# Delta-rule decay rows: a column turned with step zero instead of two fp32 products with replicated columns

## The chip, the cores and the metric

The kernel runs on one core of a Trainium2 chip, as one launch. The metric is the time of that launch on the device in microseconds, the median of several runs. Everything is float32, and matrix products are done either on plain fp32 operands or, in the projections and experts, as three products of rounded high and low parts.

## What is computed

Two layers on 512 tokens of width 1024, each a mixer and a mixture of 16 experts. The mixer of the first layer holds, beside a gated linear attention, a gated delta rule of 4 heads of width 128 in chunks of 64 tokens. The change lies there:

```
def gated_delta_chunked(q, k, v, g, beta):
    b = jnp.cumsum(g, axis=-1)
    ...
    gamma = jnp.exp(jnp.where(incl, b[..., :, None] - b[..., None, :], -jnp.inf))
    k_beta = k * beta[..., None]
    a_low = jnp.where(strict, jnp.einsum('bhnid,bhnjd->bhnij', k_beta, k) * gamma, 0.0)
    ...
    sol = lax.linalg.triangular_solve(eye + a_low, rhs, left_side=True, lower=True, unit_diagonal=True)
    ...
    qk = jnp.einsum('bhnid,bhnjd->bhnij', q, k) * gamma
    q_dec = q * jnp.exp(b)[..., None]
```

The norms of q and k are folded into the exponents: the kernel keeps log factors lk, lq and lbk (for k, q, and beta times k) per token and head. The matrix under the exponential, for token j on the partitions and token i along the row, is (b_i + lbk_i) + (lk_j - b_j) for the triangular system and (b_i + lq_i) + (lk_j - b_j) for q·k. The part with j is a column, which VectorE adds as a scalar per partition (`colj`). The part with i is needed as a row that is the same on all 128 partitions. These are the decay rows.

## The kernel before, in words

The kernel is written per engine: TensorE, VectorE (`dve`), ScalarE (`act`), GpSimd (`pool`) and SyncE (`sp`, which issues most DMAs) each run their own program in the order of the code, and named semaphores tell one engine that another has done a step. Between stages every compute engine counts up `phase_done` and waits for all (a barrier). Tokens are handled in 4 tiles of 128 (two chunks each, t = 0..3), and each tile has 4 heads, so that a tile of 4 x 128 columns fills one PSUM bank.

The delta-rule stage begins at the barrier `phase_done` 3 * 2. Ahead of it, within the linear-attention stage, `gdn_pre_gates` and `gdn_pre` (VectorE, L2211 to L2239) make the per-token columns: the log factors, and from a product of g with the triangular constant `tri` the running sums b, of which `pre[:, 1]` = b + lbk and `colj` = lk - b are kept.

The stage's own order of work:

- `gdn_inverses` (all 4 tiles). VectorE writes, per tile, g and lbk replicated over 128 columns per head into xx and xt (L2320, L2321). TensorE makes the decay rows of each tile, two fp32 products per head that add up in one bank (replicated g times `tri`, L1136; replicated lbk times identity, L1137), then k·k of the tile (L1140). VectorE adds colj and a mask (L2325, the decay step), ScalarE takes the exponential, VectorE multiplies by k·k (L2331) and makes first operands for all four tiles (L2334, L2337, L2341). TensorE turns x0 (L937, called at L1145), then five levels of inverse products follow (L1155, L1160, L1163) with VectorE's updates (L2348, L2350, L2351) and side sums for the modulation (L2062).
- `gdn_rows(0)`, `gdn_kq(0)`, `gdn_kv(0)`, `gdn_solve(0)`: decay rows of tile 0 for q·k (L1170, L1171), q·k (L1178), turned k and v (L937), and the solve (L1193, L1195). The replicated columns for these rows are made by ScalarE (`gdn_rep`, L1761 to L1768). VectorE clears ku_b (L2866), then waits for the turned k and v (L2385).
- `gdn(t)`, t = 0..3, the recurrence over two chunks c. On TensorE per chunk: product with the state (L1228), something that prepares tile t+1 (for c = 0 `gdn_rows(t + 1)`, for c = 1 `gdn_kv(t + 1)`), then the state's update (L1246), which waits for VectorE's vn (L2415). VectorE then forms the new state (L2423). ScalarE's `gdn(t)` runs the sums of squares of tile t-1 (`gdn_root`), the exponentials and copies of tile t+1, and `gdn_rep(t + 2)` at the end.

At the stage's end stands the barrier 3 * 3, after which SP starts to fetch the experts' weights (L765) and TensorE starts the output projection (L1286).

The helper `turn(dst, src)` (L936) is TensorE's transpose of src with the identity: src is the stationary operand that is loaded, the identity the moving one. In the profile names a product's moving operand comes first, so a turn of a tile in `work` reads `ps<-const,work`. All of ScalarE's activations are issued by one helper line, L1576.

Of the kernel before, what the change touches and what calls it, by code (L numbers as in the profile page):

```python
# [15 lines left out]
P = 128  # L16
SEQ, D = 512, 1024
TT = SEQ // P
# [98 lines left out]
def build_block(nc, a, out):  # L117
    ctx = ExitStack()
    with ctx:
        def sem(name):  # L120
            return ctx.enter_context(nc.semaphore(name))
# [154 lines left out]
        tiles, levels = range(TT), range(1, 6)  # L276
        MAT_PE = Steps(sem("gdn_mat_pe"), [f"{n}{t}" for t in tiles for n in ("rows", "kk")] + [f"x0{t}" for t in tiles])
        MAT_ACT = Steps(sem("gdn_mat_act"), [f"{n}{t}" for n in ("exp", "x0") for t in tiles])
        MAT_DVE = Steps(sem("gdn_mat_dve"), [f"{n}{t}" for n in ("rep", "d", "at", "level0", "xt0", "level1") for t in tiles])
        INV_PE = Steps(sem("gdn_inv_pe"), [f"{n}{l}{t}" for l in levels for n in ("p", "y") for t in tiles])  # L280
        INV_ACT = Steps(sem("gdn_inv_act"), [f"p{l}{t}" for l in levels for t in tiles])
        INV_DVE = Steps(sem("gdn_inv_dve"), [f"{n}{l}{t}" for l in levels for t in tiles
                                             for n in (("xt", "x", "level") if l < 5 else ("xt", ))])

        GDP_PE = Steps(sem("gdn_prep_pe"), ["rows", "kq", "kv", "uw"])
        GDP_ACT = Steps(sem("gdn_prep_act"), ["rep", "exp", "eq", "wT", "u"])
        GDP_DVE = Steps(sem("gdn_prep_dve"), ["kb", "vb", "d", "qk", "qd", "ku"])
        GDN_DVE = Steps(sem("gdn_dve"), ["vn0", "s0", "vn1", "s1"])
        GDH_DVE = Steps(sem("gdn_norm_dve"), ["zg", "var", "n1", "n2", "n3", "rstd", "on"])
# [134 lines left out]
        gla_end = top["work"]  # L424

        top["work"] = 0
        rep = carve("work", 2, HEADS, P)
        ex = carve("work", HEADS, P)
        xt = carve("work", TT, HEADS, P)
        kb_b = carve("work", HEADS, P)  # L430
# [14 lines left out]
        pzb = carve("work", TT, 512)  # L445
        psm = carve("work", TT, 24)
        qkvT = carve("work", 12, 3 + SEQ)
        pre_u = carve("work", TT, 8)
        pre_a = carve("work", TT, 8)
        pre_l = carve("work", TT, 8)  # L450
# [174 lines left out]
        def cols(t):  # L625
            return slice(P * t, P * t + P)
# [306 lines left out]
        def _(pe):  # L933
# [197 lines left out]

            def gdn_inverses():
                for t in range(TT):
                    pe.wait_ge(MAT_DVE.sem, MAT_DVE.at(0, f"rep{t}"))
                    for hd in range(HEADS):
                        mm(bank(t)[:, cols(hd)], xx[:, t, hd], cst("tri"), start=True, stop=False)  # L1136
                        ins = mm(bank(t)[:, cols(hd)], xt[:, t, hd], ident, start=False, stop=True)  # L1137
                    ins.then_inc(MAT_PE.sem, MAT_PE.one(f"rows{t}"))
                    for hd in range(HEADS):
                        ins = mm(bank(4 + t)[:, cols(hd)], qkvT[:, 4 + hd, tok(t)], qkvT[:, 4 + hd, tok(t)], start=True, stop=True)  # L1140
                    ins.then_inc(MAT_PE.sem, MAT_PE.one(f"kk{t}"))
                for t in range(TT):
                    pe.wait_ge(MAT_DVE.sem, MAT_DVE.at(0, f"xt0{t}"))
                    for hd in range(HEADS):
                        ins = turn(bank(t)[:, cols(hd)], xt[:, t, hd])  # L1145
                    ins.then_inc(MAT_PE.sem, MAT_PE.one(f"x0{t}"))
                for l in range(1, 6):
                    for t in range(TT):
                        if l == 1:
                            pe.wait_ge(MAT_ACT.sem, MAT_ACT.at(0, f"x0{t}"))  # L1150
                            pe.wait_ge(MAT_DVE.sem, MAT_DVE.at(0, f"level1{t}"))
                        else:
                            pe.wait_ge(INV_DVE.sem, INV_DVE.at(0, f"level{l - 1}{t}"))
                        for hd in range(HEADS):
                            ins = mm(bank(t)[:, cols(hd)], lev_at[:, t, hd], xx[:, t, hd], start=True, stop=True)  # L1155
                        ins.then_inc(INV_PE.sem, INV_PE.one(f"p{l}{t}"))
                    for t in range(TT):
                        pe.wait_ge(INV_ACT.sem, INV_ACT.at(0, f"p{l}{t}"))
                        for hd in range(HEADS):
                            ins = mm(bank(4 + t)[:, cols(hd)], pm[:, t, hd], xt[:, t, hd], start=True, stop=True)  # L1160
                        if l < 5:
                            for hd in range(HEADS):
                                ins = mm(bank(t)[:, cols(hd)], xt[:, t, hd], pm[:, t, hd], start=True, stop=True)  # L1163
                        ins.then_inc(INV_PE.sem, INV_PE.one(f"y{l}{t}"))
                pe.wait_ge(INV_DVE.sem, INV_DVE.at(0, f"xt5{TT - 1}"))

            def gdn_rows(t):
                pe.wait_ge(GDP_ACT.sem, GDP_ACT.at(t, "rep"))
                for hd in range(HEADS):
                    mm(bank(1)[:, cols(hd)], rep[:, 0, hd], cst("tri"), start=True, stop=False)  # L1170
                    ins = mm(bank(1)[:, cols(hd)], rep[:, 1, hd], ident, start=False, stop=True)  # L1171
                ins.then_inc(GDP_PE.sem, GDP_PE.one("rows"))

            def gdn_kq(t):
# [399 lines left out]
        def _(act):  # L1574
            def f(out, in_, fn=ACT.Copy, **kw):
                return nc.scalar.activation(out, in_, fn, **kw)  # L1576
# [181 lines left out]
                            act.wait_ge(INV_PE.sem, INV_PE.at(0, f"y{l - 1}{t}"))  # L1758
                        f(pm[:, t], bank(t, HEADS, P)).then_inc(INV_ACT.sem, INV_ACT.one(f"p{l}{t}"))

            def gdn_rep(t):  # L1761
                if t:
                    act.wait_ge(GDP_PE.sem, GDP_PE.at(t - 1, "rows"))
                else:
                    act.wait_ge(PRE_DVE.sem, PRE_DVE.at(0, "lq"))
                for n, src in enumerate((g_b, lq)):
                    ins = f(rep[:, n], src[:, t].unsqueeze(2).to_broadcast([P, HEADS, P]))
                ins.then_inc(GDP_ACT.sem, GDP_ACT.one("rep"))  # L1768

            def gdn_prep(t):  # L1770
                b = t % 2
                act.wait_ge(GDP_DVE.sem, GDP_DVE.at(t, "d"))
# [22 lines left out]
            def gdn(t):  # L1795
                ahead = t + 1 < TT
                if t:
                    gdn_root(t - 1)
                if ahead:
                    table(ACT.Exp)  # L1800
                    gdn_prep(t + 1)
                else:
                    put_mod(0, 0, 4)
                if t:
                    put_output_b(t - 1)
                if ahead:
                    gdn_solve(t + 1)
                if t + 2 < TT:
                    gdn_rep(t + 2)
                if ahead:  # L1810
                    table(ACT.Abs_reciprocal_sqrt)

# [177 lines left out]
            gla()  # L1990
            nc.scalar.drain().then_inc(phase_done, 1)
            act.wait_ge(phase_done, 3 * 2)
            gdn_rep(0)
            table(ACT.Exp)
            gdn_inverses()
            gdn_prep(0)
            gdn_solve(0)
            gdn_rep(1)
            for t in range(TT):
                gdn(t)  # L2000
            gdn_root(TT - 1)
# [32 lines left out]
        def _(dve):  # L2034
# [194 lines left out]
            def gdn_pre():  # L2229
# [3 lines left out]
                v.tensor_copy(pre[:, 0], lnb)  # L2233
                v.tensor_tensor(pre[:, 1], cum[:, 0], lbk, ALU.add)
                v.tensor_tensor(pre[:, 2], cum[:, 1], lk, ALU.add)
                v.tensor_copy(pre[:, 3:5], cum[:, 2:4]).then_inc(D_.sem, D_.one("pre"))
                v.tensor_tensor(colj, lk, cum[:, 0], ALU.subtract).then_inc(D_.sem, D_.one("colj"))
                dve.wait_ge(D_.sem, D_.at(0, "colj"))
# [77 lines left out]

            def gdn_inverses():

                for t in range(TT):
                    v.tensor_copy(xx[:, t], g_b[:, t].unsqueeze(2).to_broadcast([P, HEADS, P]))  # L2320
                    v.tensor_copy(xt[:, t], lbk[:, t].unsqueeze(2).to_broadcast([P, HEADS, P])).then_inc(MAT_DVE.sem, MAT_DVE.one(f"rep{t}"))  # L2321
                for t in range(TT):
                    dve.wait_ge(MAT_PE.sem, MAT_PE.at(0, f"rows{t}"))
                    for hd in range(HEADS):
# [606 lines left out]
```

## Time and profile before

| | us |
|---|---|
| median of 3 runs | 1470.79 |
| lowest, highest | 1470.17, 1473.98 |
| span of the profiled execution | 1464.9 |
| TensorE busy in it | 1280.1 (87%) |
| VectorE busy | 1101.5 (75%) |
| ScalarE busy | 693.7 (47%) |
| mean granted TensorE clock | 0.924 |
| delta-rule stage in it, from its barrier to the next | about 309 to 449 |

The span runs from the first to the last instruction of one profiled execution; for the profiled execution no other time is given than its span, which lies 5.9 us below the median of the runs. Matmuls are pipelined: the records of successive ones overlap, so the distance from start to start is the pace, not a record's length. An fp32 product of this size shows as two records, a turn as one. In a timeline, neighbouring instructions of one line are put together: start, time to the last one's end, how many records, and in brackets the idle time ahead with what ended it.

### The profile page before, as it was taken

What the parts mean: (1) busy time and instruction counts of PE and PEld (TensorE: products, weight loads), DVE (VectorE), ACT (ScalarE), POOL (GpSimd) and SP (SyncE); (2) the same over time, 40 slices, a digit from 0 to 9 for tenths busy, and PEclk for the clock granted to TensorE, in tenths of its full rate; (3) what the DMA queues carried; (4) which work ended last, traced back from release to release, by engine and by line L of the source; (5) the groups of instructions that cost most, each with busy time, mean ns of one, the idle gap of its engine ahead of it and who ended that gap; (6) DMA issues with size and microseconds to landing.
All of it is one profiled execution on the core that took longest, in us unless ns stands there. A gap on an engine that the chain in (4) does not pass through costs nothing. (4 is left out here: it accounts for less than half of the span.)

```text
span 1464.9 us, 15502 instructions
## 1 busy us (share of the span) xinstructions
PE 1280.1 (87%) x6000; PEld 970.2 (66%) x6000; DVE 1101.5 (75%) x1324; ACT 693.7 (47%) x890; POOL 311.9 (21%) x129
## 2 busy tenths in 40 slices
PE   4798997859899959999999967986898799999992
PEld 1476885659884557888888754444446588888882
DVE  2757986667783657999999946967357499999994
ACT  2222344222251316777777714227522377777770
POOL 2100000000000001555555310000000145555541
PEclk9799998979999959999999977997996799999997
DMA  9788626011703257999999546354006499999955
GB/s 328 259 266 272 214 96 211 19 44 58 259 2 130 87 219 273 375 391 382 373 378 373 225 157 240 115 203 183 1 29 258 142 358 385 377 381 392 380 206 191
DMA packets 63856, 338.17 MB, mean 231 GB/s; under 512 B 11837, under 2 KB 12350, under 8 KB 49700
## 3 DMA queue, kind: packets, MB, share of 16 engines
q1 hardware_dynamic: 51428, 311.00, 57.3%
q0 software_dynamic: 11536, 22.91, 4.5%
q10 hardware_dynamic: 816, 3.23, 0.6%
q8 instruction: 50, 0.82, 0.2%
q14 instruction: 26, 0.21, 0.0%
HBM read 325.64 MB, written 28.84 MB: 242 GB/s over the span
## 5 line engine op out<-in xcount | busy, mean ns | idle before, releaser
L1421 PE MATMUL ps<-ring_r,work_r 128*128 128x512 f32 x536 | 212.7, 397 | 0.0
L2455 DVE TENSOR_TENSOR ring_r<-ring,early_mod_r 128x2048 fp32r<-128x2048 f32 x76 | 188.7, 2512 | 21.2 <-ACT early_mod_r L1576 20.7
L1419 PE MATMUL ps<-early_mod_r,work_r 128*128 128x512 f32 x468 | 187.8, 401 | 7.7 <-DVE work_r L2758 4.7
L834 POOL TENSOR_TENSOR work<-work,early_mod 128x1024 f32<-128x1024 f32 x30 | 158.1, 5271 | 157.3 <-ACT work L1576 157.3
L1576 ACT ACTIVATE work<-ps 128x512 f32<-128x512 f32 (+3 forms) x121 | 80.5, 670 | 224.8 <-PE ps L1421 134.7
L1420 PE MATMUL ps<-early_mod_r,work_r 128*128 128x512 f32 x468 | 183.1, 391 | 0.0
L1576 ACT ACTIVATE work_r<-ring 128x2048 fp32r<-128x2048 f32 (+2 forms) x87 | 133.8, 1558 | 89.2 <-PE ps L946 89.2
L1576 ACT ACTIVATE early_mod_r<-ring 128x2048 fp32r<-128x2048 f32 x79 | 147.6, 1910 | 0.3 <-PE ps L1421 0.3
L937 PE MATMUL ps<-const,work 128*128 128x128 f32 x712 | 106.4, 293 | 44.2 <-DMA work<-h_rows,row_i 11.9
L1419 PE MATMUL ps<-work_r 128*128 128x512 f32 x324 | 132.9, 410 | 6.8 <-DVE work_r L2758 4.7
L937 PEld LDWEIGHTS ps<-const,work 128*128 128x128 f32 x712 | 90.1, 151 | 68.7 <-issue 15.0
L2455 DVE TENSOR_TENSOR ring_r<-ring,work_r 128x2048 fp32r<-128x2048 f32 x52 | 130.4, 2533 | 1.1 <-ACT work_r L1576 1.1
L1420 PE MATMUL ps<-work_r 128*128 128x512 f32 x324 | 128.9, 398 | 0.0
L1421 PEld LDWEIGHTS ps<-ring_r,work_r 128*128 128x128 f32 x536 | 102.7, 192 | 23.1
L1286 PE MATMUL ps<-ring,hT 128*128 128x512 f32 x256 | 111.1, 593 | 1.4 <-ACTq L2025 0.7
L1419 PEld LDWEIGHTS ps<-early_mod_r,work_r 128*128 128x128 f32 x468 | 88.2, 188 | 29.0 <-DVE work_r L2758 8.1
L1420 PEld LDWEIGHTS ps<-early_mod_r,work_r 128*128 128x128 f32 x468 | 88.4, 189 | 17.0
L826 POOL DMA_INDIRECT work<-h_rows,row_i x32 | 57.3, 1790 | 177.9 <-PE ps L937 130.1
L1286 PEld LDWEIGHTS ps<-ring,hT 128*128 128x128 f32 x256 | 48.2, 190 | 60.8 <-issue 58.3
L1310 PE MATMUL ps<-ring,hT 128*128 128x512 f32 x192 | 86.2, 608 | 1.9 <-ACT hT L1576 1.9
L1576 ACT ACTIVATE work_r<-ps 128x512 fp32r<-128x512 f32 (+1 forms) x66 | 53.3, 810 | 66.4 <-PE ps L937 66.4
L1419 PEld LDWEIGHTS ps<-work_r 128*128 128x128 f32 x324 | 62.7, 194 | 23.0 <-DVE work_r L2758 7.7
(330 smaller groups left out, 2448.3 us busy)
## 6 DMA issues: line engine op xcount, KB each, us to landing
ring<-in_moe_w_up_dram SPq DMA_DIRECT2D x33, 2048.0 KB, 10.8
early_mod<-in_ada_w_dram SPq DMA_DIRECT2D x80, 512.0 KB, 4.4
ring<-in_moe_w_gate_dram SPq DMA_DIRECT2D x19, 2048.0 KB, 9.6
hT<-in_moe_w_down_dram SPq DMA_DIRECT2D x16, 2048.0 KB, 9.9
ring<-in_moe_w_down_dram SPq DMA_DIRECT2D x15, 2048.0 KB, 10.2
work<-in_moe_w_gate_dram SPq DMA_DIRECT2D x14, 2048.0 KB, 10.8
ring<-in_ab_w_in_dram SPq DMA_DIRECT2D x7, 2048.0 KB, 10.4
ring<-in_ada_w_dram SPq DMA_DIRECT2D x4, 2048.0 KB, 23.6
```

Of the source, the lines that this page charges most:

```text
L826: nc.gpsimd.indirect_dma_start(xg[buf], None, h_rows[l], bass.IndirectOffsetOnAxis(rows_, 0), bounds_check=SEQ - 1, oob_is_err=False).then ...
L834: return nc.gpsimd.tensor_tensor(yb[buf], yb[buf], mod[:, 5 * D:6 * D], ALU.mult)
L937: return nc.tensor.transpose(dst, src, ident[0:k, 0:k])
L1286: ins = mm(bank((2 * t + n) % 3), oT[:, k, cols(t)], slot(c0 + n)[:, k], start=(k == 0), stop=(k == 7))
L1310: ins = mm(bank(j % 4), hT[:, k, cols(t)], slot(c)[:, k], start=(k == 0), stop=(k == 7))
L1419: mm(out, a_lo, w_hi, start=first_, stop=False)
L1420: mm(out, a_hi, w_hi, start=False, stop=False)
L1421: return mm(out, a_hi, w_lo, start=False, stop=last_)
L1576: return nc.scalar.activation(out, in_, fn, **kw)
L2455: v.tensor_tensor(half_of(l, m, half, True), half_of(l, m, half), highs[(2 * m + half) % MHIGHS].bitcast(F32), ALU.subtract).then_inc(SV.s ...
```

## The change

The decay rows are made otherwise. `pre[:, 1]`, the column b + lbk per token and head, exists already; a new column `colq` = b + lq is made beside it with one addition. A decay row tile for a head is then the transpose of a 128 x 128 view of that single column, read with step zero along the columns: `turn(bank, column.to_broadcast([P, P]))`. This replaces the two fp32 products per head in `gdn_inverses` (16 heads x tiles) and in `gdn_rows` (another 16). The replicated copies go: eight of VectorE's in `gdn_inverses`, and the eight activations of ScalarE's `gdn_rep`, with the waits of TensorE for both. The tile `rep` is no longer carved; `colq` lies in free columns of `psm`.

```diff
-        MAT_DVE = Steps(sem("gdn_mat_dve"), [f"{n}{t}" for n in ("rep", "d", "at", "level0", "xt0", "level1") for t in tiles])
+        MAT_DVE = Steps(sem("gdn_mat_dve"), [f"{n}{t}" for n in ("d", "at", "level0", "xt0", "level1") for t in tiles])
...
-        GDP_ACT = Steps(sem("gdn_prep_act"), ["rep", "exp", "eq", "wT", "u"])
+        GDP_ACT = Steps(sem("gdn_prep_act"), ["exp", "eq", "wT", "u"])
...
-        rep = carve("work", 2, HEADS, P)
...
+        colq = psm[:, :, 0:HEADS]
...
             def gdn_inverses():
                 for t in range(TT):
-                    pe.wait_ge(MAT_DVE.sem, MAT_DVE.at(0, f"rep{t}"))
                     for hd in range(HEADS):
-                        mm(bank(t)[:, cols(hd)], xx[:, t, hd], cst("tri"), start=True, stop=False)
-                        ins = mm(bank(t)[:, cols(hd)], xt[:, t, hd], ident, start=False, stop=True)
+                        ins = turn(bank(t)[:, cols(hd)], pre[:, 1, t, hd:hd + 1].to_broadcast([P, P]))
...
             def gdn_rows(t):
-                pe.wait_ge(GDP_ACT.sem, GDP_ACT.at(t, "rep"))
                 for hd in range(HEADS):
-                    mm(bank(1)[:, cols(hd)], rep[:, 0, hd], cst("tri"), start=True, stop=False)
-                    ins = mm(bank(1)[:, cols(hd)], rep[:, 1, hd], ident, start=False, stop=True)
+                    ins = turn(bank(1)[:, cols(hd)], colq[:, t, hd:hd + 1].to_broadcast([P, P]))
...
-            def gdn_rep(t):
-                if t:
-                    act.wait_ge(GDP_PE.sem, GDP_PE.at(t - 1, "rows"))
-                else:
-                    act.wait_ge(PRE_DVE.sem, PRE_DVE.at(0, "lq"))
-                for n, src in enumerate((g_b, lq)):
-                    ins = f(rep[:, n], src[:, t].unsqueeze(2).to_broadcast([P, HEADS, P]))
-                ins.then_inc(GDP_ACT.sem, GDP_ACT.one("rep"))
-
...
-                if t + 2 < TT:
-                    gdn_rep(t + 2)
...
-            gdn_rep(0)
...
-            gdn_rep(1)
...
                 v.tensor_tensor(pre[:, 2], cum[:, 1], lk, ALU.add)
+                v.tensor_tensor(colq, cum[:, 0], lq, ALU.add)
...
             def gdn_inverses():
 
-                for t in range(TT):
-                    v.tensor_copy(xx[:, t], g_b[:, t].unsqueeze(2).to_broadcast([P, HEADS, P]))
-                    v.tensor_copy(xt[:, t], lbk[:, t].unsqueeze(2).to_broadcast([P, HEADS, P])).then_inc(MAT_DVE.sem, MAT_DVE.one(f"rep{t}"))
```

TensorE in the recurrence at t = 0, from the product with the state to its update, before. Behind a line stands the semaphore it waits for: `gdn_prep_act` is ScalarE's, `gdn_prep_dve` and `gdn_dve` are VectorE's.

```order
L1228 MATMUL ps<-work,ring 64x128 [waits gdn_prep_act]
L1228 MATMUL ps<-work,ring 64x128 x3
L1170 MATMUL ps<-early_mod,work 128x128 [waits gdn_prep_act]
L1171 MATMUL ps<-const,work 128x128
...
L1246 MATMUL ps<-work,ring 128x128 [waits gdn_prep_dve,gdn_dve]
L1246 MATMUL ps<-work,ring 128x128 x3
```

The same place in the changed kernel, whose line numbers are 4 lower (L1228 is L1224 there, L1246 is L1242):

```order
L1224 MATMUL ps<-work,ring 64x128 [waits gdn_prep_act]
L1224 MATMUL ps<-work,ring 64x128 x3
L937 MATMUL ps<-const,work 128x128 x4
L1242 MATMUL ps<-work,ring 128x128 [waits gdn_prep_dve,gdn_dve]
L1242 MATMUL ps<-work,ring 128x128 x3
```

Eight products with a wait for ScalarE have become four turns with none; nothing else stands between the two lines.

## Rows read from the trace of the kernel before

**Rows 1.** Timeline, ScalarE then VectorE at the barrier (start us, us, engine line op)
```profile
308.53 0.60 ACT L1576 ACTIVATE hT<-ps 128x512 f32<-128x512 f32 x1 [0.43 <-PE ps L937]
309.29 1.15 ACT L1576 ACTIVATE work<-work 128x512 f32<-128x512 f32 x2 [0.17 <-ACTq L1991]
...
309.87 0.48 DVE L2863 MEMSET work<- 128x512 f32 x1
310.39 0.43 DVE L2320 COPY ring<-work 128x512 f32<-128x512 f32 x1
```

**Rows 2.** Timeline, TensorE in the first decay rows and k·k
```profile
311.30 0.76 PE L1136 MATMUL ps<-early_mod,ring 128*128 128x128 f32 x2 [2.81 <-DVE work L2321]
...
314.84 1.91 PE L1140 MATMUL ps<-work 128*128 128x128 f32 x8
316.55 0.60 PE L1136 MATMUL ps<-early_mod,ring 128*128 128x128 f32 x2
...
323.91 1.06 PE L1140 MATMUL ps<-work 128*128 128x128 f32 x8
```

**Rows 3.** Timeline, VectorE, decay steps of the first and last tile
```profile
315.09 1.12 DVE L2325 SCALAR_TENSOR_TENSOR ring<-ps,work,early_mod 128x128 f32<-128x128 f32 x4 [1.92 <-PE ps L1137]
...
324.11 1.12 DVE L2325 SCALAR_TENSOR_TENSOR ring<-ps,work,early_mod 128x128 f32<-128x128 f32 x4 [1.55 <-PE ps L1137]
325.15 1.28 DVE L2331 TENSOR_TENSOR ring<-ps,ring 128x512 f32<-128x512 f32 x2
```

**Rows 4.** Windows of 1 us: engines' busy time, then PEclk, DMA share, GB/s
```profile
316.00:317.00 1.00, 1.00 (x7) 1.00 (x7) 0.21 (x1) 0.63 (x1) 0.00 (x0) 0.51 0.00 0
317.00:318.00 1.00, 1.00 (x11) 1.00 (x11) 0.00 (x0) 0.00 (x0) 0.00 (x0) 1.00 0.00 0
...
333.00:334.00 1.00, 1.00 (x7) 1.00 (x6) 1.00 (x3) 0.75 (x2) 0.00 (x0) 0.50 0.00 0
334.00:335.00 1.00, 1.00 (x11) 1.00 (x10) 0.84 (x2) 0.74 (x2) 0.00 (x0) 0.98 0.00 0
```

**Rows 5.** Timeline, TensorE then VectorE, decay rows of tile 0 for q·k
```profile
385.07 0.49 PE L1170 MATMUL ps<-early_mod,work 128*128 128x128 f32 x2 [0.78 <-DVE work L2348]
...
387.86 1.04 PE L937 MATMUL ps<-const,work 128*128 128x128 f32 x8
...
385.39 1.76 DVE L2866 MEMSET ring<- 128x2048 f32 x1 [0.38 <-issue]
388.93 0.69 DVE L2385 TENSOR_TENSOR work<-ps,work 128x512 f32<-128x512 f32 x1 [1.77 <-PE ps L937]
```

**Rows 6.** Timeline, TensorE then VectorE, recurrence at t = 0 and 1
```profile
394.53 0.49 PE L1170 MATMUL ps<-early_mod,work 128*128 128x128 f32 x2 [0.43 <-ACT work L1576]
...
396.42 1.06 PE L1246 MATMUL ps<-work,ring 128*128 128x128 f32 x8
...
408.95 1.06 PE L1246 MATMUL ps<-work,ring 128*128 128x128 f32 x8
...
394.67 0.68 DVE L2415 TENSOR_TENSOR work<-ring,ps 64x512 f32<-64x512 f32 x1
...
407.57 0.68 DVE L2415 TENSOR_TENSOR work<-ring,ps 64x512 f32<-64x512 f32 x1
408.93 0.17 DVE L2394 TENSOR_SCALAR work<-work 128x4 f32<-128x4 f32 x1 [0.68 <-ACT early_mod L1576]
```

**Rows 7.** Timeline, TensorE, turns of x0 and first inverse products
```profile
330.69 3.58 PE L937 MATMUL ps<-const,work 128*128 128x128 f32 x16 [5.72 <-DVE work L2337]
334.11 3.73 PE L1155 MATMUL ps<-ring 128*128 128x128 f32 x32
```

**Rows 8.** Timeline, VectorE, end of the decay preparation
```profile
261.52 0.16 DVE L2237 TENSOR_TENSOR work<-work,ps 128x16 f32<-128x16 f32 x1
263.48 1.28 DVE L2062 SCALAR_TENSOR_TENSOR x<-early_mod,par,x 128x1024 f32<-128x1024 f32 x1 [1.80 <-issue]
```

**Rows 9.** Timeline, SP's queue, first expert weights
```profile
448.83 0.33 SPq L765 DMA_DIRECT2D ring<-in_moe_w_gate_dram  x1
```

## The prediction

> **What bounds the kernel now.** I read the views from the outside in. The chain that ended last covers only the final DMA and adds, so it says nothing of this stage; I took the windows table and then the timeline of each engine over the delta-rule stage, from about 309 us to 449 us of the span. What matters there is which wait ends last at each of the four places where decay rows are made.
>
> At the entry, ScalarE's last copy of the stage before starts at 308.53 and takes 0.60, and its next work starts at 309.29 [rows 1]. That barrier releases everybody. VectorE then clears two tiles and writes eight replicated tiles (L2320, L2321); TensorE's first product starts at 311.30, released by the first L2321 [rows 1, 2]. So 2 us pass between barrier and product, for operands only. Then TensorE is the bound: the decay step of VectorE (L2325) is idle before each tile and released by L1137 each time; the last tile's step starts at 324.11, and everything behind it on VectorE is back to back [rows 3]. The pitch is slow because the granted clock is 0.50 until 317, 1.00 after [rows 4], that is 1.2 and then 2.4 GHz, 5.7 us after the first product.
>
> At the second place, TensorE makes the decay rows of tile 0 (L1170, L1171) from 385.07, then queues k·q and the turned k and v behind them; VectorE has finished clearing ku_b (385.39 + 1.76 = 387.15) and waits 1.77 us for the turned k and v [rows 5]. In the loop, the rows of tile t+1 stand between the product with the state (L1228) and the state's update (L1246) on TensorE. They start at 394.53 after waiting 0.43 us for ScalarE's replica and the update starts at 396.42, whereas VectorE had its operand at 394.67 + 0.68 [rows 6].
>
> **The change part by part.** The price of the new operation first. A turned 128x128 tile is one record where an fp32 product is two: 8 turns take 1.04 us at full clock with the last one's tail, 0.11 us each, and the 16 from 330.69 to the next line's 334.11 at half clock, 0.21 us each [rows 5, 7]. Two fp32 products are 4 records: the eight products of a tile take 394.53 to 396.42, 1.89 us with 0.1 us of entry [rows 6]. So one tile's decay rows go from 1.79 us to 0.45 us at full clock, 0.85 us at half clock. No row shows a turn whose source has step zero. From below it can't cost less than the 0.11 us pitch, since the identity still streams through the array; from above the nearest rows are these ordinary turns, and the farthest the products it replaces, 0.45 us per head. I take the ordinary turn. The Trainium skill (SBUF — State Buffer, Door 1: The DMA port swizzle) says repeated accesses to one 16-byte line run at full bandwidth, which a step of zero would satisfy; no run here shows it yet.
>
> *Entry and first rows.* VectorE's eight copies and TensorE's wait for them go. TensorE starts at 309.4 instead of 311.30 (0.1 us after the barrier at 309.3). In front of the last decay step stand 4 groups of turns and 3 groups of k·k; a k·k group is 1.71 us at half clock (314.84 to 316.55) and 0.9 us at full (eight of the 32 records that take 3.73 us) [rows 2, 7]. At half clock throughout this is 4 x 0.85 + 3 x 1.71 + 0.4 of pipeline tail = 8.9 us, so the last step starts at 318.3: 5.8 us earlier than 324.11. If the clock rises 5.7 us after the first turn, as it did here, the 2.8 us of work left shrink to 1.5, it starts at 316.8: 7.3 us earlier. If it rises 3.4 us after (as it did behind the turns of 330.69, below), at 315.8: 8.3 us earlier. TensorE was last busy just before the barrier, closer than now, so I take the middle of the last two, **7.8 us**. VectorE isn't a new bound: tile 0's rows are ready at 310.65, after its two clears (309.87 + 0.48 = 310.35), and a step of 1.12 us per tile is shorter than TensorE's 1.3 to 2.6 us per tile [rows 1, 3].
>
> *Second climb of the clock.* Between the stages TensorE waits 5.72 us for VectorE and starts the turns of x0 at half clock; 3.4 us later the clock is up [rows 4, 7]. After the change the distance may be anything from 3.4 to 5.7 us, and up to 2.3 us of work at half clock costs up to 1.1 us more. I take **0.5 us back**.
>
> Here the trace contradicts a rule. Between 324.97 and 334 TensorE did nothing but 16 turns, and the window 333 to 334 shows 0.50, 334 to 335 shows 0.98 [rows 4, 7]: turns alone had raised the clock. The Trainium skill (TensorE: Matmul & The Clock Gate, Part 4: PE-mode transpose) says that transposes don't count as busy and the fast clock doesn't engage for them. The row decides for the sum; by the rule it would be 7.3 us (rival A).
>
> *Rows of tile 0.* 1.79 - 0.45 = **1.34 us**. Whole, because VectorE's cover, the clearing of ku_b, ends 1.77 us before the operands come [rows 5].
>
> *Loop, tiles 1, 2, 3.* Here VectorE's vn takes over as what ends last, so the 1.34 us don't count whole. For t = 0 the update starts at 394.67 + 0.68 + 0.05 = 395.40 instead of 396.42: **1.02 us** (TensorE's rows would be done at 394.4). For t = 1 vn starts at 407.57, so the update starts at 408.30 instead of 408.95: **0.65 us** [rows 6]. The next turn of the loop has the same pattern 12.9 us later (one more **0.65 us**). The last has no rows to make. ScalarE loses its replicas (two activations of 1.15 us together, four times), and so begins its sums of squares earlier; before, VectorE waited 0.68 us for them at 408.93, after vn and before the update's result [rows 6]. The update's result now comes at 408.30 + 1.06 = 409.36, still behind that addition's end at 409.10, and without the replica ScalarE is 1.15 us earlier besides. It costs nothing.
>
> *Added.* One VectorE addition, colq, of the kind of L2237 (0.16 us), in the decay preparation. VectorE is idle for 1.80 us right behind it, waiting for ScalarE's exponentials [rows 8]; if that cover were gone, it would cost 0.1 us.
>
> Sum: 7.8 - 0.5 + 1.34 + 1.02 + 0.65 + 0.65 = 11.0 us. It reaches the end, since SP issues the first expert weights at 448.83, behind the barrier that ends this stage [rows 9], so the whole weight stream moves with it. The side weights fetched in the stage are paced by VectorE's own use of them. The profiled execution has a span of 1464.9 us, and the median of the runs shown is 5.9 us above that, so I subtract from the median: 1470.8 - 11.0 = **1459.8 us**, or 1453.9 us of span.
>
> **The rivals.**
> *A, the clock stays low in the first stage.* k·k is half or more of the work there and might be broken up too much by turns. Then the first term is 5.8. If the turns of x0 don't raise it either, the inverse products behind them run at half clock for the 3.4 to 5.7 us that a climb takes, which costs half of that, 2.2 us in the middle: 5.8 - 2.2 + 3.66 = 7.3 us, 1463.5 us. For it: the first climb took 5.7 us here with products alone; against it: turns alone made the second [rows 2, 4, 7]. 8%.
> *B, it isn't worth what it frees.* The gain is there at 449 us but is lost in later stages to clock climbs that fall otherwise, each at most some 1 us as above; it would take seven of them to come below 4.4 us. The three runs differ by 3.8 us. About 1467. 5%.
> *C, slower: the weight load with step zero.* All 128 columns of a load read one address of each partition. If that serialises, a turn's load no longer hides under the products. All 32 turns stand in TensorE's queue ahead of a waiting engine. The 11.0 us are gone when each costs 0.34 us more, some 0.45 to 0.55 us for a turn, four times the ordinary one; at eight times, 0.9 us, it would be 32 x 0.79 - 11 = 14 us slower, 1485 us. For it: only that no row shows such a read. Against: VectorE reads such columns to make the replicas at 0.43 us for 512 elements, under 1 ns each [rows 1]. 3%.
> That the change doesn't do what it says: TensorE could still wait at the entry, for ScalarE's drain, which the 309.3 already holds; the rows of the loop lose their wait altogether. Included in B.
>
> **How the numbers follow.** The forecast has 84%, within itself 1458.5 to 1462.4 by its bounds (5.8 - 1.1 + 3.66 = 8.4 at the least, 8.3 + 3.66 = 12.0 at the most). With the runs' scatter, and with A, the range is 1457.0 to 1464.3. About 0.3%, 4.4 us, is what a measurement can tell from no change. Faster by more: forecast and A, 0.91. Same: B and the near part of C, 0.06. Slower: 0.03.
>
> **What would show it.** Right: the first turn near 309.4; 16 records of decay rows in the first stage and 16 later, in place of 64 and 64; the last decay step starting near 316; VectorE's idle time before kb shrunk from 1.77 to 0.4 us; the update L1246 released by VectorE and no longer following rows back to back; barrier to SP's first expert load near 438. Wrong: turns further apart than 0.11 us at full clock or loads longer than the ordinary turn's (C); the window from 314 to 318 still at 0.50 (A); SP's load at 438 with an end not 11 us earlier (B).

## The result, and the profile after

The changed kernel takes 1457.38 us (median of 4 runs, 1455.11 to 1460.33) against 1470.48 us for the kernel before (4 runs). The ratio is 0.9909, 95% interval 0.9884 to 0.9933: faster, by 10 to 17 us. The forecast was 1459.8 us in a range of 1457.0 to 1464.3.

| | before, us | after, us |
|---|---|---|
| span of the profiled execution | 1464.9 | 1453.1 |
| TensorE busy | 1280.1 | 1271.0 |
| VectorE busy | 1101.5 | 1098.0 |
| ScalarE busy | 693.7 | 689.7 |
| stage: VectorE's clearing of vn to the output projection's first product | 139.46 | 128.51 |

The stage counts for the whole gain, to within what traces scatter by: the two spans differ by 11.8 us, of which 10.95 lie in the stage, 1.50 ahead of it, and the part behind it is 0.65 longer. Here is the timeline of TensorE in the changed kernel at the entry, which answers to [rows 2, 7]. Columns are start and length in us, engine, line, operands, number of records, and in brackets the idle time ahead with what ended it.

```profile
307.71 1.12 PE L937 MATMUL ps<-const,work 128*128 128x128 f32 x4 [0.72 <-ACTq L1976]
308.62 1.92 PE L1138 MATMUL ps<-work 128*128 128x128 f32 x8
310.33 1.06 PE L937 MATMUL ps<-const,work 128*128 128x128 f32 x4
311.18 1.47 PE L1138 MATMUL ps<-work 128*128 128x128 f32 x8
312.48 0.60 PE L937 MATMUL ps<-const,work 128*128 128x128 f32 x4
312.92 1.06 PE L1138 MATMUL ps<-work 128*128 128x128 f32 x8
313.81 0.60 PE L937 MATMUL ps<-const,work 128*128 128x128 f32 x4
314.25 1.06 PE L1138 MATMUL ps<-work 128*128 128x128 f32 x8
321.03 3.67 PE L937 MATMUL ps<-const,work 128*128 128x128 f32 x16 [5.72 <-DVE work L2318]
324.49 4.31 PE L1153 MATMUL ps<-ring 128*128 128x128 f32 x32
```

TensorE starts 0.7 us behind its last turn of the stage before, released by ScalarE's drain (`ACTq`), and not by a VectorE copy. From start to start four turns take 0.85 to 0.91 us at half clock and 0.44 us at full. The last two rows show the other side: the turns of x0 again start 5.72 us after TensorE went idle, again at half clock.

VectorE at the same place, the counterpart of [rows 1, 3]:

```profile
307.83 0.48 DVE L2843 MEMSET work<- 128x512 f32 x1 [2.01 <-ACTq L1976]
308.37 0.48 DVE L2844 MEMSET work<- 128x512 f32 x1
308.93 1.12 DVE L2306 SCALAR_TENSOR_TENSOR ring<-ps,work,early_mod 128x128 f32<-128x128 f32 x4
311.43 1.13 DVE L2306 SCALAR_TENSOR_TENSOR ring<-ps,work,early_mod 128x128 f32<-128x128 f32 x4 [1.37 <-PE ps L937]
313.12 1.13 DVE L2306 SCALAR_TENSOR_TENSOR ring<-ps,work,early_mod 128x128 f32<-128x128 f32 x4 [0.57 <-PE ps L937]
314.45 1.13 DVE L2306 SCALAR_TENSOR_TENSOR ring<-ps,work,early_mod 128x128 f32<-128x128 f32 x4 [0.20 <-PE ps L937]
```

The first decay step finds its rows ready; the later ones wait less and less, 1.37, 0.57, 0.20 us, where before the four waited 1.92, 2.53, 1.55 and 1.55. TensorE is still the bound, but hardly. The last step starts 6.62 us behind the clearing of vn, before it was 14.78 us (324.11 - 309.33, the start of the first of the two clearings).

The windows of 1 us (engines' busy time, then PEclk, DMA share, GB/s), the counterpart of [rows 4]:

```profile
311.00:312.00 1.00, 1.00 (x6) 1.00 (x5) 0.57 (x3) 0.00 (x0) 0.00 (x0) 0.50 0.13 53
312.00:313.00 1.00, 1.00 (x11) 1.00 (x10) 0.55 (x3) 0.41 (x1) 0.00 (x0) 0.99 0.00 0
...
319.00:320.00 1.00, 0.00 (x0) 0.00 (x0) 1.00 (x3) 0.00 (x0) 0.00 (x0) 0.50 0.00 0
...
325.00:326.00 1.00, 1.00 (x8) 1.00 (x8) 0.18 (x1) 0.34 (x1) 0.00 (x0) 0.66 0.08 16
326.00:327.00 1.00, 1.00 (x12) 1.00 (x11) 0.00 (x0) 0.60 (x1) 0.00 (x0) 1.00 0.00 0
```

The clock rises 4.3 us behind the first turn, between the 3.4 and 5.7 us that bounded the estimate, and the second time some 4.6 us behind the first turn of x0.

Tile 0 and the recurrence, TensorE then VectorE, the counterpart of [rows 5, 6]:

```profile
376.03 0.65 PE L937 MATMUL ps<-const,work 128*128 128x128 f32 x4 [0.78 <-DVE work L2329]
...
383.59 0.65 PE L937 MATMUL ps<-const,work 128*128 128x128 f32 x4
384.96 1.16 PE L1242 MATMUL ps<-work,ring 128*128 128x128 f32 x8 [0.72 <-DVE work L2396]
...
396.95 1.16 PE L1242 MATMUL ps<-work,ring 128*128 128x128 f32 x8 [0.59 <-DVE work L2396]
...
376.35 1.76 DVE L2847 MEMSET ring<- 128x2048 f32 x1 [0.38 <-issue]
378.49 0.69 DVE L2366 TENSOR_TENSOR work<-ps,work 128x512 f32<-128x512 f32 x1 [0.37 <-PE ps L937]
...
396.22 0.68 DVE L2396 TENSOR_TENSOR work<-ring,ps 64x512 f32<-64x512 f32 x1
396.82 0.15 DVE L2375 TENSOR_SCALAR work<-work 128x4 f32<-128x4 f32 x1
```

VectorE's wait for the turned k and v is 0.37 us, from 1.77. The state's update L1242 now waits for VectorE's vn (L2396): the bound has changed hands, as forecast. At that place the variance step (L2375) no longer waits for ScalarE; its fourth and last occurrence still waits 1.73 us, as before. The end of the stage, in SP's queue:

```profile
436.38 0.33 SPq L765 DMA_DIRECT2D ring<-in_moe_w_gate_dram  x1
```

Laid side by side, in pieces that add up to the stage (each from start to start in the timelines):

| piece, us | before | after | measured | forecast |
|---|---|---|---|---|
| clearing of vn to last decay step | 14.78 | 6.62 | -8.16 | -7.8 |
| to TensorE's first update product of the inverses (L1160) | 13.57 | 14.19 | +0.62 | +0.5 |
| to VectorE's last inverse update (L2348) | 46.65 | 46.65 | 0 | 0 |
| to kb of tile 0 (L2385) | 4.60 | 3.20 | -1.40 | -1.34 |
| to the state's first update (L1246) | 7.49 | 6.47 | -1.02 | -1.02 |
| to the first update at t = 2 | 25.44 | 24.36 | -1.08 | -1.30 |
| to the output projection | 26.93 | 27.02 | +0.09 | 0 |
| sum | 139.46 | 128.51 | -10.95 | -10.96 |

### The profile page after: what moved, and what is told of

Read it like the earlier page. It is cut to its first block and busy times, and to the rows that moved or that the text cites. A ratio compares the mean times of both kernels' runs of the same rounds, so it can differ in the third digit from the quotient of the medians.

```text
span 1453.1 us, 15293 instructions
## 1 busy us (share of the span) xinstructions
PE 1271.0 (87%) x5904; PEld 960.4 (66%) x5904; DVE 1098.0 (76%) x1317; ACT 689.7 (47%) x882; POOL 310.5 (21%) x129
## 5 line engine op out<-in xcount | busy, mean ns | idle before, releaser
L2436 DVE TENSOR_TENSOR ring_r<-ring,early_mod_r 128x2048 fp32r<-128x2048 f32 x76 | 193.2, 2572 | 23.7 <-ACT early_mod_r L1572 23.2
L834 POOL TENSOR_TENSOR work<-work,early_mod 128x1024 f32<-128x1024 f32 x30 | 150.4, 5014 | 151.9 <-ACT work L1572 151.9
L937 PE MATMUL ps<-const,work 128*128 128x128 f32 x744 | 114.7, 298 | 45.6 <-DMA work<-h_rows,row_i 11.9
L937 PEld LDWEIGHTS ps<-const,work 128*128 128x128 f32 x744 | 96.0, 153 | 70.8 <-issue 14.9
L2436 DVE TENSOR_TENSOR ring_r<-ring,work_r 128x2048 fp32r<-128x2048 f32 x52 | 126.2, 2451 | 3.4 <-ACT work_r L1572 3.4
L826 POOL DMA_INDIRECT work<-h_rows,row_i x32 | 62.8, 1961 | 186.1 <-PE ps L937 138.1
L830 POOL DMA_INDIRECT y_rows<-work,dest_i x32 | 71.1, 2222 | 34.5 <-POOL work L834 23.2
## 6 DMA issues: line engine op xcount, KB each, us to landing
ring<-in_ab_w_in_dram SPq DMA_DIRECT2D x7, 2048.0 KB, 10.1
```

What stands on the lines that cost most here:

```text
L826: nc.gpsimd.indirect_dma_start(xg[buf], None, h_rows[l], bass.IndirectOffsetOnAxis(rows_, 0), bounds_check=SEQ - 1, oob_is_err=False).then ...
L830: nc.gpsimd.indirect_dma_start(y_rows[l], bass.IndirectOffsetOnAxis(rows_, 0), yb[buf], None, bounds_check=2 * SEQ - 1, oob_is_err=False). ...
L834: return nc.gpsimd.tensor_tensor(yb[buf], yb[buf], mod[:, 5 * D:6 * D], ALU.mult)
L937: return nc.tensor.transpose(dst, src, ident[0:k, 0:k])
L2436: v.tensor_tensor(half_of(l, m, half, True), half_of(l, m, half), highs[(2 * m + half) % MHIGHS].bitcast(F32), ALU.subtract).then_inc(SV.s ...
```

## The experiments

Every run below is told by the same two pieces that vary (to the last decay step, and from there to the first update product of the inverses) and by the stage. before_again, products_step0, dense_turns, turns_x4, fill_turns and fill_products were executed once each and are read from their traces alone. A single time is no guide here: products_step0 took 1465.59 us and the kernel before, once beside it, 1463.70, although the stage of products_step0 is 2 us shorter than in either trace of the kernel before.

**The same two kernels once more.** No edit.

> The changed kernel once more, to part the stage from the scatter around it. The stage is counted from VectorE's clearing of vn to the first product of the output projection: 139.46 us before, 128.51 us changed. Theory A (the whole gain is in the stage): the stage is again 128.5 within 1 us, the run 11 us faster than before (ratio 0.9925), and the 1.6 us by which the barrier came earlier in the first trace is scatter, so here it may come anywhere from 307 to 310 us. Theory B (some of the gain lies ahead of the stage, through shorter programs): the barrier is again near 307.7 us and the run 12.5 to 13 us faster (ratio 0.991).

> The kernel before once more, for its trace alone. Theory A: stage 139.5 within 1 us, the clock's first climb anywhere from 3.4 to 5.7 us behind the first product, which moves the stage by up to 1 us; the barrier anywhere from 307 to 310 us. Theory B: barrier again near 309.3 us.

The changed kernel: 6.69, 14.22, stage 128.62 us; ratio 0.9931, interval 0.9915 to 0.9946. The kernel before: 13.70, 14.81, stage 139.61 us. The clearing of vn came at 311.57 and 310.35 us. So A holds: the lead of 1.5 us ahead of the stage in the first trace of the changed kernel isn't its doing, since the second trace has it 3.7 us later. It also shows that the two pieces trade with one another. In the second trace of the kernel before the first is 1.1 us shorter and the second 1.2 us longer, because the clock rose at another point (it is 1.00 from 309.5 to 312.5 us, 0.50 again from 313, and 1.00 again from 316.5); the sum hardly moves.

**Each part alone.** The replicas and the waits for them go with their products.

```diff
 inverses_only: the kernel before, with
-                        mm(bank(t)[:, cols(hd)], xx[:, t, hd], cst("tri"), start=True, stop=False)
-                        ins = mm(bank(t)[:, cols(hd)], xt[:, t, hd], ident, start=False, stop=True)
+                        ins = turn(bank(t)[:, cols(hd)], pre[:, 1, t, hd:hd + 1].to_broadcast([P, P]))
 rows_only: the kernel before, with
-                    mm(bank(1)[:, cols(hd)], rep[:, 0, hd], cst("tri"), start=True, stop=False)
-                    ins = mm(bank(1)[:, cols(hd)], rep[:, 1, hd], ident, start=False, stop=True)
+                    ins = turn(bank(1)[:, cols(hd)], colq[:, t, hd:hd + 1].to_broadcast([P, P]))
```

> Only the decay rows of the triangular systems are turned columns; those of q times k stay fp32 products with ScalarE's replicas. Theory A (the terms are independent waits in one chain): the stage loses 8.1 - 0.6 = 7.5 us and is 132.0 us (131 to 133); ratio 0.995. Rival (the two parts overlap, so that either alone brings most of it): stage 129 to 130 us.

> Only the decay rows of q times k are turned columns; VectorE's eight replicas and the products in the triangular systems stay. Theory A: 1.40 us at tile 0, 1.02, 0.65 and 0.65 in the loop, less 0.1 us for each of three updates that now start from an idle TensorE: 3.4 us, stage 136.0 us (135.5 to 137, by the clock's climb); ratio 0.9977. Rival (VectorE's chain sets the loop, so only tile 0 counts): stage 138.0 us.

inverses_only: stage 131.78 us, 7.68 us shorter; ratio 0.9944 (0.9926 to 0.9962). rows_only: stage 136.04 us, 3.42 us shorter; ratio 0.9978 (0.9967 to 0.9988). Together 11.10 us, against 10.95 for both at once. Piece by piece it holds too. Behind the first two pieces inverses_only has the kernel before's lengths, each within 0.02 us (4.60, 7.49, 25.45, 26.92). rows_only has the kernel before's first two (14.77, 13.56) and then the changed kernel's (3.20, 6.48, 24.35, 27.03). The terms are separate waits in one chain and add; neither rival holds.

**Operand or operation?** The products stay, but read g and lbk (or lq) with step zero, so that nobody writes replicas.

```diff
-                        ins = turn(bank(t)[:, cols(hd)], pre[:, 1, t, hd:hd + 1].to_broadcast([P, P]))
+                        mm(bank(t)[:, cols(hd)], g_b[:, t, hd:hd + 1].to_broadcast([P, P]), cst("tri"), start=True, stop=False)
+                        ins = mm(bank(t)[:, cols(hd)], lbk[:, t, hd:hd + 1].to_broadcast([P, P]), ident, start=False, stop=True)
```

> No replicas, but the two fp32 products per head stay, with the columns of g and lbk (or lq) themselves read with step zero as the stationary operand. It parts the operand's wait from the operation's price. Theory (the price counts for most): TensorE starts right behind the barrier, 1.9 us earlier than before, and the wait of 0.43 us at t = 0 is gone, so the stage is 139.5 - 2.3 = 137.1 us (136 to 138 by the clock's climb). Rival (what mattered was the wait for replicas): stage under 132 us. Rival C of the prediction (a step-zero weight load is slow): products further apart than 0.11 us a record at full clock, loads longer than 0.19 us, stage longer than 139.5 us.

Measured: 12.03, 14.84, stage 137.48 us, and 0.50 us shorter at t = 0. So in these traces 2.0 us of the 10.95 come from not writing replicas, and 9 us from the cheaper operation. The waits themselves were 2.6 us (the first product starts 0.12 us ahead of the clearing, before 1.97 behind it, and 0.50 at t = 0). The other 0.6 us went to where the clock rose, so the split is good to about that. The groups of this kernel's weight loads, minimum/median/maximum in ns:

```profile
L1135 PEld LDWEIGHTS ps<-early_mod,work x32: 190/192/334, 309.1 to 320.6; 128*128 128x128 f32 x32
L1135 PE MATMUL ps<-early_mod,work x32: 275/275/579, 309.1 to 320.7; 128*128 128x128 f32 x32
```

and of the kernel before, whose operands are dense:

```profile
L1136 PEld LDWEIGHTS ps<-early_mod,ring x32: 192/193/334, 311.3 to 323.5; 128*128 128x128 f32 x32
L1136 PE MATMUL ps<-early_mod,ring x32: 274/275/551, 311.3 to 323.6; 128*128 128x128 f32 x32
```

A load of one column read 128 times lasts as long as a load of 128 columns.

**A dense tile to turn.** VectorE writes b + lbk replicated, one copy per tile, and TensorE turns that.

```diff
-                        ins = turn(bank(t)[:, cols(hd)], pre[:, 1, t, hd:hd + 1].to_broadcast([P, P]))
+                        ins = turn(bank(t)[:, cols(hd)], xx[:, t, hd])
...
+                    v.tensor_copy(xx[:, t], pre[:, 1, t].unsqueeze(2).to_broadcast([P, HEADS, P])).then_inc(MAT_DVE.sem, MAT_DVE.one(f"rep{t}"))
```

> In the triangular systems VectorE writes the finished column b + lbk replicated over 128 columns (one copy per tile), and TensorE turns that dense tile; the rows of q times k stay turned step-zero columns. Theory (a step-zero load costs what a dense one costs): the turns keep their pitch of 0.21 us at half and 0.11 us at full clock; the first one starts 1.5 us behind the clearing of vn instead of at it, and the stage is 1.5 us longer than the changed kernel's, 130.0 us (129.3 to 130.8). Rival (step zero is slower than dense): it gives back part of that and is 129 us or less.

Measured: 7.93, 14.31, stage 129.97 us, 1.46 us above the changed kernel, as expected. It is made of a first turn that comes 1.75 us later, of 0.44 us won back up to the last decay step, since the clock happened to be up for the first turns (1.00 until 310.4 us), and of 0.15 us behind that step. The rows of the turns themselves are the cleaner evidence. At full clock, dense first, then step zero in the changed kernel:

```profile
L937 PEld LDWEIGHTS ps<-const,ring x8: 140/141/146, 313.9 to 315.6; 128*128 128x128 f32 x8
L937 PE MATMUL ps<-const,ring x8: 272/273/273, 314.0 to 315.7; 128*128 128x128 f32 x8
```

```profile
L937 PEld LDWEIGHTS ps<-const,work x8: 137/137/139, 312.4 to 314.0; 128*128 128x128 f32 x8
L937 PE MATMUL ps<-const,work x8: 272/272/273, 312.5 to 314.1; 128*128 128x128 f32 x8
```

137 against 141 ns: step zero costs nothing. Rival C of the prediction falls with these two runs.

**The price of a turn by dose.** The result is the same; each group is only done four times, here and in `gdn_rows`.

```diff
+                    for _ in range(4):
                         for hd in range(HEADS):
                             ins = turn(bank(t)[:, cols(hd)], pre[:, 1, t, hd:hd + 1].to_broadcast([P, P]))
```

> Each group of four step-zero turns is done four times over into the same bank, the same result each time. Theory (0.21 us a turn at half clock, 0.11 us at full, all on the path in the first stage and at tile 0, and hidden behind VectorE's vn for part of it in the loop): in the triangular systems 48 more turns, about 0.21 us each until the clock has climbed and 0.11 us after, 6.5 us together; tile 0 1.34 us; the loop 1.34 - 0.97 = 0.6, then 2 x 0.75 us: the stage is 10 us longer, about 138.5 us (137 to 140). Rival (loads of one address pile up when they follow closely): more than 142 us.

Measured: 9.80, 13.43, stage 133.48 us: 5.0 us longer than the changed kernel, half of what I expected, and a miss. Of the 5 us that are missing, 3.3 lie ahead of the last decay step, 0.8 in the second piece (the clock's second climb fell better), and 0.9 in the loop, where VectorE's vn hides more than I had put down. For the first part, I had reckoned the first turns at half clock. In this run the clock had risen to 1.00 ahead of the barrier, and stayed:

```profile
309.50 1.96 PE L937 MATMUL ps<-const,work 128*128 128x128 f32 x16 [0.72 <-ACTq L1978]
311.30 1.06 PE L1139 MATMUL ps<-work 128*128 128x128 f32 x8
312.19 1.91 PE L937 MATMUL ps<-const,work 128*128 128x128 f32 x16
313.94 1.06 PE L1139 MATMUL ps<-work 128*128 128x128 f32 x8
```

16 turns in 1.75 to 1.80 us are 0.11 us each, the price that the forecast used. Against the first piece at full clock without extra turns (4.56 us, fill_both below) the 48 more cost 5.24 us, 0.109 us each; at tile 0 the 12 more cost 1.31 us, and in the loop 0.43 to 0.46 us per tile, since 0.9 us of the 1.34 fits under VectorE's vn. Step-zero loads that follow each other 16 times don't pile up.

**Do turns keep the clock up?** 44 turns of the identity fill TensorE's idle time ahead of the turns of x0; their bank is overwritten afterwards.

```diff
+                pe.wait_ge(MAT_DVE.sem, MAT_DVE.at(0, "d{}".format(TT - 1)))
+                for n_ in range(44):
+                    turn(bank(0)[:, cols(n_ % HEADS)], ident)
                 for t in range(TT):
                     pe.wait_ge(MAT_DVE.sem, MAT_DVE.at(0, f"xt0{t}"))
```

> The changed kernel with 44 turns of the identity in TensorE's idle time between the last product of k with k and the turns of x0, into a bank that is overwritten afterwards. They do nothing but keep TensorE going. Theory T (turns count as work for the clock, as the 16 turns at 330.69 us of the kernel before suggest): the granted clock stays at 1.00 up to the turns of x0, the first inverse level ends 1.6 us earlier and the stage is 127.0 us (126.5 to 127.6). Rival R (the rule that transposes don't count): the clock falls to 0.50 in the gap as before and the stage is 128.5 us or longer.

Measured: 6.77, 12.72, stage 127.19 us. TensorE in this kernel:

```profile
319.90 5.03 PE L937 MATMUL ps<-const 128*128 128x128 f32 x44 [0.33 <-DVE ring L2309]
325.30 2.46 PE L937 MATMUL ps<-const,work 128*128 128x128 f32 x16 [0.37 <-DVE work L2321]
327.80 3.81 PE L1156 MATMUL ps<-ring 128*128 128x128 f32 x32
```

and its clock at the place where the changed kernel had 0.50:

```profile
324.00:325.00 1.00, 0.92 (x9) 0.68 (x7) 1.00 (x3) 0.00 (x0) 0.00 (x0) 1.00 0.00 0
326.00:327.00 1.00, 1.00 (x8) 0.73 (x8) 1.00 (x3) 1.00 (x2) 0.00 (x0) 1.00 0.00 0
```

Theory T: turns count. This settles the rule that the prediction weighed. The Trainium skill (TensorE: Matmul & The Clock Gate, Part 4: PE-mode transpose) says that transposes don't count as busy for the fast clock; here nothing but turns ran between 319.9 and 327.8, and the clock stayed at 1.00 throughout, whereas without them it fell. The measurement decides, for fp32 turns as in this kernel.

**The same, timed, and with fillers ahead of the barrier too.** fill_turns_timed is that kernel again, after_third the changed kernel on the same chip, and fill_both adds:

```diff
+                for n_ in range(36):
+                    turn(bank(7)[:, cols(n_ % HEADS)], ident)
                 for t in range(TT):
                     pe.wait_ge(GLN_DVE.sem, GLN_DVE.at(0, f"on{t}"))
...
+                    if t + 1 < TT:
+                        for n_ in range(4):
+                            turn(bank(7)[:, cols(n_ % HEADS)], ident)
```

> The changed kernel, timed on the same chip as the next two so that they can be set against it: ratio to before 0.9925 (0.991 to 0.994), stage 128.5 us within 1 us.

> The changed kernel with 44 idle-time turns ahead of the turns of x0, timed. Theory T: stage 127.2 us again, so 1.4 us below the changed kernel in the median as well (ratio to before 0.9915). Rival (the power that the extra turns draw is given back by a lower clock later on): the stage is shorter and the median isn't.

> As before, and with 36 turns of the identity ahead of the last turns of the linear-attention stage and 4 between each two groups of them, so that the clock is up when the delta-rule stage begins. Theory T: the granted clock is 1.00 from the barrier on, the last decay step starts 4.75 us behind the clearing of vn instead of 6.6 us, the stage is 125.2 us (124.8 to 125.9), and the barrier itself is some 0.3 us earlier; ratio to before 0.990. Rival (VectorE's decay steps become the bound, 1.04 us each from 1.1 us on): last step at 4.2 us at the earliest, which is no limit here; if the fillers hold up the real turns, the barrier comes later by what they overrun.

| | pieces, us | stage, us | median, us | ratio to before |
|---|---|---|---|---|
| after_third | 6.73, 14.24 | 128.70 | 1456.20 | 0.9930 (0.9907 to 0.9954) |
| fill_turns_timed | 4.56, 12.73 | 125.01 | 1451.39 | 0.9894 (0.9866 to 0.9923) |
| fill_both | 4.56, 12.73 | 125.00 | 1452.21 | 0.9908 (0.9879 to 0.9936) |

fill_both does what it should: the clock is 1.00 through the barrier, and the stage is 125.0 us. The real turns ahead of the barrier aren't held up: from the first of them to the first turn of the stage it takes 4.47 us, in the changed kernel 4.93. VectorE's decay steps of the first three tiles now run back to back, and only the last still waits:

```profile
308.58 3.30 DVE L2314 SCALAR_TENSOR_TENSOR ring<-ps,work,early_mod 128x128 f32<-128x128 f32 x12
312.08 1.12 DVE L2314 SCALAR_TENSOR_TENSOR ring<-ps,work,early_mod 128x128 f32<-128x128 f32 x4 [0.20 <-PE ps L937]
```

The profiled execution of fill_turns_timed reached the same 125.0 us without the second filler, because its clock happened to be up at the barrier (0.99 in the half microsecond from 307.0); in fill_turns, the same kernel, it wasn't, and the stage was 127.2 us. My expectation of 127.2 missed here, because it left that case out. Both medians lie 4 to 5 us below the changed kernel's, with intervals that overlap its own and each other's. The traces show 3.7 us; the times agree with that but don't prove it by themselves, nor do they tell the two fillers apart. Nothing shows that the fillers' gain is given back by a lower clock later on: the mean granted clocks of their twelve executions are 0.924 to 0.932, those of after_third 0.921 to 0.927.

**Products as filler.** 22 fp32 products in place of the 44 turns, the loop shortened to 22.

```diff
-                    turn(bank(0)[:, cols(n_ % HEADS)], ident)
+                    mm(bank(0)[:, cols(n_ % HEADS)], ident, ident, start=True, stop=True)
```

> As fill_turns, with 22 fp32 products of the identity in place of the 44 turns: the same number of records. If turns and products count alike for the clock, the stage is the same, 127.2 us; if turns count for less, this one keeps the clock up where turns only sometimes do, and is up to 0.5 us shorter.

Measured: 6.71, 12.72, stage 127.14 us. The same as with turns: with the same number of records, turns and products held the clock up alike across this gap.

## Why the prediction was right

*Entry and first rows, 7.8 us.* Measured 8.16. The steps hold one by one: first turn at 307.71, right behind the barrier; 0.85 to 0.91 us per group; the clock's climb at 4.3 us, between the two bounds that I took the middle of. VectorE didn't become the bound. Of this term, products_step0 shows that 2.1 us are the operand's wait. That the middle was close is in part luck. Between before_again and after_again the same term measures 7.01 us. In the six traces whose rows were turned columns and whose clock wasn't up at the barrier, the climb came 4.1 to 4.6 us behind the first turn. The case that it is up already, worth 2.1 us more, wasn't in the prediction.

*Second climb, 0.5 us back.* Measured 0.62 in the first pair of traces, but between before_again and after_again this piece became 0.59 us shorter. Only the sum of the two terms is steady: 7.54 us in the first pair, 7.60 in the second, 7.3 forecast. The fillers show what is at stake: with the clock up throughout, the piece is 12.72 us instead of 14.19.

*Rows of tile 0, 1.34 us.* Measured 1.40, and again in rows_only.

*Loop, 1.02 + 0.65 + 0.65 us.* The starts are as forecast. What I left out is that an update which now starts on an idle TensorE lasts 1.16 us from its start instead of 1.06 (L1242 above, L1246 in [rows 6]). That takes 0.1 us back three times, in the two pieces 25.44 to 24.36 and 26.93 to 27.02. The same extra length stood in the other rows with idle time ahead of them, such as L1170's 0.49 us in [rows 5].

*Added, nothing.* VectorE's idle time behind the decay preparation went from 1.80 us [rows 8] to 1.72:

```profile
262.00 1.28 DVE L2045 SCALAR_TENSOR_TENSOR x<-early_mod,par,x 128x1024 f32<-128x1024 f32 x1 [1.72 <-issue]
```

*The sum and the median.* 10.95 us in the stage against 10.96 on paper; errors of 0.3 us cancelled, so the match to 0.01 us is luck. The first measurement's medians differ by 13.1 us, more than the 12.0 that the prediction's own bounds allow at most (its 1458.5 should be 1458.8), and 1457.38 lies within 0.4 us of the range's lower end, which only the allowance for scatter covers. The repeats give less: the medians of after_again differ by 8.8 us (10.1 by its ratio), those of after_third by 10.3. All three intervals hold 11.0. The 2 us beyond the sum are most likely scatter outside the stage: over all traces the clearing of vn comes anywhere from 307.5 to 312.2 us, and what follows the stage lasts from 1010.5 to 1020.3 us, with no order by kernel.

*Rivals.* A (the clock stays low): in the changed kernel it rose from 0.50 to 1.00 at 312.0, among turns and k·k, and fill_turns speaks against the rule behind it. B (lost later): what the repeats measure agrees with the whole 11 us, though their intervals are 5 to 7 us wide; no trace shows a loss behind the stage. C (a slow step-zero load): products_step0 and dense_turns measure no such cost. Its price counted all 32 turns in full, but in turns_x4 only a third of what was added in the loop came out as time.

## What to carry to other kernels

A value per partition that is needed as a row on all partitions is one transpose of its column read with step zero: half the records of an fp32 product against the identity, and no replica to write, wait for or keep. If the value was a running sum made by multiplying a replica by a triangle, make the sum once as a column and turn that. Where TensorE idles for a few microseconds in front of a chain that it bounds, look at the granted clock on the far side; turns of a constant into a free bank kept it up here, at 0.11 us each.

## What the runs showed that I had not expected

The clock at the barrier isn't the same in every execution of one kernel. Of the thirteen traces without the entry filler (before, after, and eleven of the runs), four had risen ahead of the barrier, during the four spaced groups of turns: before_again, dense_turns, turns_x4 and fill_turns_timed. What happened next went with the gap. In before_again TensorE then waited 2.81 us for the replicas, and the clock fell again:

```profile
309.00:310.00 1.00, 0.51 (x3) 0.20 (x1) 0.00 (x0) 0.66 (x2) 0.00 (x0) 0.86 0.00 0
311.00:312.00 1.00, 0.00 (x0) 0.00 (x0) 0.96 (x3) 0.98 (x2) 0.02 (x1) 1.00 0.07 20
313.00:314.00 1.00, 1.00 (x6) 1.00 (x6) 1.00 (x4) 0.00 (x0) 0.00 (x0) 0.50 0.39 156
```

In dense_turns it waited 2.47 us, and the clock fell at 310.4. In turns_x4 and fill_turns_timed it waited only 0.72 us, and the clock stayed at 1.00. These are two traces against two. They suggest that the replicas cost more than their 2 us in such executions, since starting at once also keeps a clock that is up. In time that is worth 2.1 us, the difference between first pieces of 6.7 and 4.56 us; before_again, where it fell, had a stage of 139.61 us and gained nothing from it.
